# Expert stage of a hybrid encoder layer: plain fp32 products in 64-row blocks in place of split products in 80-row blocks, a ring of six weight sets, the residual kept in SBUF

## The reference, cut to what matters

```python
D_MODEL, N_GROUPS, EXPERTS_PER_GROUP, TOP_K, D_EXPERT = 1024, 4, 8, 2, 256
...
x = x + mix                                   # x2 below
t = rmsnorm(x, norm2_g).reshape(-1, D_MODEL)  # 576 rows
lg = t @ w_rg + b_rg                          # group; the best one is taken
le = t @ w_re + b_re                          # experts; the best two of that group
combine = ...                                 # (576, 32), two entries per row
def step(acc, xs):
    wg, wu, wd, c = xs                        # (1024,256) (1024,256) (256,1024)
    hdn = jax.nn.silu(t @ wg) * (t @ wu)
    return acc + c[:, None] * (hdn @ wd), None
x = x + acc
y = rmsnorm(x, final_g)
```

## Time and profile before

| | |
|---|---|
| median of 3 executions | 1424.2 us (1412.7 to 1426.9) |
| span of the profiled execution, its only time shown | 1420.8 us |
| PE busy | 1264.7 us, 89% of the span |
| DVE, ACT, POOL busy | 796.2, 616.8, 67.5 us |
| read from and written to HBM | 181.3 and 31.0 MB |

### The profile page before, as it was taken

The page is one execution under the profiler, slowest core; times in us unless marked ns, Lnnn a source line. Parts: engine busy times, 40 slices in busy tenths (PEclk is TensorE's granted clock), DMA queues, the critical chain, the costliest instruction groups (busy, mean ns, idle before and its releaser), DMA issues.

```text
span 1420.8 us, 22301 instructions
## 1 busy us (share of the span) xinstructions
PE 1264.7 (89%) x8549; PEld 1130.7 (80%) x8549; DVE 796.2 (56%) x938; ACT 616.8 (43%) x819; POOL 67.5 (5%) x132
## 2 busy tenths in 40 slices
PE   5989999999999999999989989982788888888880
PEld 4989999999999999999989989982455555555550
DVE  4437374473755736547365444326567677677645
ACT  5434243343433434335343222232566666666632
POOL 0001010010100101001010000003000000000002
PEclk9999999999999999999999999965799999999995
DMA  5261121211121112121102235533888888888836
GB/s 186 95 208 54 58 71 61 72 47 61 65 67 56 61 61 65 53 71 61 63 22 80 80 103 164 211 136 127 293 319 322 321 323 325 316 329 328 313 126 220
DMA packets 49434, 212.80 MB, mean 150 GB/s; under 512 B 5920, under 2 KB 8496, under 8 KB 37104
## 3 DMA queue, kind: packets, MB, share of 16 engines
q1 hardware_dynamic: 41200, 194.05, 39.2%
q0 software_dynamic: 2928, 10.05, 2.1%
q10 hardware_dynamic: 5264, 8.13, 1.6%
HBM read 181.25 MB, written 30.96 MB: 149 GB/s over the span
## 4 chain that ended last, share of the span: by engine, by line
PE 78%; DVE 7%; ACT 6%; DMA 4%; issue 3%; POOL 1%; SPq 0%; ACTq 0%; DVEq 0%; POOLq 0%
PE proj L620 25%; PE proj L1337 15%; PE wideB L1358 6%; PE proj L987 5%; PE wideA L378 4%; PE proj L930 3%; PE wideB L370 3%; PE wideB L384 2%; PE wideA L1324 2%; DVE xbl L1426 2%; ACT xbh L1422 2%; PE small L987 2%; DMA wraw<-in_w_in 1%; PE small L1178 1%; POOL scr_rows L1783 1%
## 5 line engine op out<-in xcount | busy, mean ns | idle before, releaser
L620 PE MATMUL proj<-xnh,whi 128*128 128x288 f32 x1152 | 347.9, 302 | 11.1 <-DVE xnl L1868 6.3
L620 PE MATMUL proj<-xnl,whi 128*128 128x288 f32 x1152 | 347.2, 301 | 0.0
L620 PE MATMUL proj<-xnh,wlo 128*128 128x288 f32 x1152 | 347.0, 301 | 0.0
L620 PEld LDWEIGHTS proj<-xnh,whi 128*128 128x128 f32 x1152 | 217.9, 189 | 12.3 <-issue 5.7
L1414 DVE TENSOR_TENSOR elo<-eraw,ehi 128x4096 fp32r<-128x4096 f32 x64 | 214.6, 3354 | 19.8 <-ACT ehi L1404 19.8
L620 PEld LDWEIGHTS proj<-xnl,whi 128*128 128x128 f32 x1152 | 217.8, 189 | 0.0
L620 PEld LDWEIGHTS proj<-xnh,wlo 128*128 128x128 f32 x1152 | 217.8, 189 | 0.0
L1337 PE MATMUL proj<-ehi,xbh 128*80 128x512 f32 x256 | 111.0, 433 | 33.9 <-DVE xbl L1426 33.9
L632 DVE TENSOR_TENSOR wlo<-wraw,whi 128x1024 fp32r<-128x1024 f32 x72 | 95.1, 1321 | 58.1 <-ACT whi L628 57.1
L1404 ACT ACTIVATE ehi<-eraw 128x4096 fp32r<-128x4096 f32 x32 | 116.1, 3627 | 0.5
L1337 PE MATMUL proj<-elo,xbh 128*80 128x512 f32 x256 | 109.9, 429 | 0.0
(11 more groups left out here) (329 smaller groups left out, 2370.2 us busy)
## 6 DMA issues: line engine op xcount, KB each, us to landing
wraw<-in_w_in SPq DMA_DIRECT2D x72, 512.0 KB, 3.3
eraw<-in_w_gate SPq DMA_DIRECT2D x32, 1024.0 KB, 4.9
eraw<-in_w_up SPq DMA_DIRECT2D x32, 1024.0 KB, 7.2
eraw<-in_w_down SPq DMA_DIRECT2D x32, 1024.0 KB, 5.5
wraw<-in_w_out SPq DMA_DIRECT2D x24, 512.0 KB, 3.7
xb<-scr_rows SPq DMA_DIRECT2D x32, 320.0 KB, 6.0
scr_y<-yout SPq DMA_DIRECT2D x32, 320.0 KB, 5.7
scr_gate<-gate ACTq DMA_DIRECT2D x16, 288.0 KB, 2.1
```

Source lines behind the costliest of these rows:

```text
L620: mm = pe.matmul(out, w[:, kc, :], x[:, kc, hh * HALF:(hh + 1) * HALF], start=(j == 0), stop=(j == 23))
```

## The change

The expert stage is rewritten; phases 1 to 3 keep their computation.

- Products are plain fp32 on the weights as loaded: per block 8 products for gate and up and 4 for down. All splitting of weights, rows and hidden values is gone; ACT copies the turned rows (`xT`), DVE the turned hidden values (`hT`).
- `BR` is 64 in place of 80. Rows and results of a block are 64 x 1024; `OVER`, the highest number of further blocks, is 17 in place of 14. The turned rows of two blocks have a place of their own in `wideA`.
- Six weight sets (`ring`) and three row buffers (`XB`). Sets 0 to 2 are loaded in phase 2, ahead of the last output weights, sets 3 and 4 at its end, set 5 behind the routing; set b mod 6 is loaded again when down of its block is done.
- `x2` stays in SBUF: its store and its five loads are gone, and the `scr_x2` array with them. Results are stored from ACT's queue.
- On PE, down of block b-1 follows the whole gate and up of block b.

```diff
-BR = 80
+BR = 64
+RING, XB = 6, 3
...
+        ring = []
+        for r, start in enumerate((0, EW, AT_RING2, AT_RING3, AT_W0, AT_P3)):
...
+            ring.append(sb(p4, f"ring{r}", [P, EW]))
...
-            weights_low(dve, 0, 0, 0)
-            weights_low(dve, 0, 0, 1)
...
+        def rows_turned(pe, b, k, x, arrived=None):
...
+            for c in range(KC):
+                mm = pe.transpose(wideA[:, 512 * k + c * BR:512 * k + (c + 1) * BR], v[:, c, :], ident[0:BR, 0:BR])
             mm.then_inc(e_xt, 1)
...
-            pe.wait_ge(e_low, 2 * b + 1)
-            pe.wait_ge(e_xl, b + 1)
+            pe.wait_ge(*(arrived or (e_w[r], 48 * (b // RING) + 48)))
+            pe.wait_ge(e_xc, b + 1)
             wait(pe, e_hid, b - 1)
...
+            for c in range(KC):
+                mm = pe.matmul(proj[k][0:BR, :], xT[k][:, c, :], w[:, :, c, :], start=(c == 0), stop=(c == KC - 1))
             mm.then_inc(e_gu, 1)
...
+            for c in range(2):
+                for n in range(2):
+                    at_w = GU + c * D + HALF_D * n
+                    mm = pe.matmul(wideB[0:BR, HALF_D * n:HALF_D * (n + 1)], hT[k][:, c, :],
+                                   ring[r][:, at_w:at_w + HALF_D], start=(c == 0), stop=(c == 1))
             mm.then_inc(e_dn, 1)
...
         def phase4_scalar(act):
...
+            rows_copied(act, 0, 0)
+            for b in range(EXPERTS):
+                silu_gate(act, b, b % 2)
+                if b > 0:
+                    y_copy(act, b - 1, (b - 1) % 2)
+                if b + 1 < EXPERTS:
+                    rows_copied(act, b + 1, (b + 1) % 2)
+                if b > 0:
+                    y_store(act, b - 1, (b - 1) % 2)
...
+            for r in range(3):
+                weights_load(r, r, e_w[r])
             sp.wait_ge(m_low, KC)
...
+            sp.wait_ge(route, ROUTE_STEPS)
+            weights_load(5, 5, e_w[5])
+            for b in range(1, EXPERTS):
+                if b + RING - 1 < EXPERTS:
+                    r = (b - 1) % RING
+                    sp.wait_ge(e_dn, b)
+                    weights_load(b + RING - 1, r, e_w[r])
+                if b + XB - 1 < EXPERTS:
+                    rows_load(b + XB - 1, (b - 1) % XB)
...
             def further(j):
...
-                sp.wait_ge(e_y, j + EXPERTS)
-                sp.dma_start(xb[0][0:BR, :], scr_rows[at(r, BR), :]).then_inc(o_x, 16)
-                gate_up_load(e, 0, o_w)
-                down_load(e, 0, o_w)
...
+                sp.wait_ge(e_dn, j + EXPERTS)
+                sp.dma_start(xb[LAST_X][0:BR, :], scr_rows[at(r, BR), :]).then_inc(o_x, 16)
+                weights_load(e, LAST_R, o_w)
```

More of the change, by code:

```diff
@@ L214, in encoder_layer @@
         a2.close()
-        a2 = area(AT_GD)
-        x2 = sb(a2, "x2", [P, UNITS, D])
+        a2 = area(AT_ML)
         ml = sb(a2, "ml", [P, KC, TOK], F32R)
         tg = [sb(a2, f"tg{k}", [P, TOK]) for k in range(2)]
-        mix = [sb(a2, f"mix{k}", [P, TOK]) for k in range(2)]
+        mix = [sb(a2, "mix0", [P, TOK]), None]
+        a2.close()
+        a2 = area(AT_G2)
+        mix[1] = sb(a2, "mix1", [P, TOK])
         a2.close()
@@ L223, in encoder_layer @@
         a2.close()
+        a2 = area(AT_X2)
+        x2 = sb(a2, "x2", [P, UNITS, D])
+        a2.close()
+        p4 = area(AT_YA)
+        xb = [sb(p4, f"xb{k}", [P, D]) for k in range(XB)]
+        xT = [sb(p4, f"xT{k}", [P, KC, BR]) for k in range(2)]
+        yout = [sb(p4, "yout0", [P, D]), None]
+        p4.close()
+        p3 = area(AT_G2)
+        g2row = sb(p3, "g2row", [P, D])
+        p3.close()
+        p3 = area(AT_YA)
+        tn = sb(p3, "tn", [P, UNITS, D])
+        p3.close()
         p3 = area(AT_P3)
-        g2row = sb(p3, "g2row", [P, D])
         wr = sb(p3, "wr", [P, KC, GROUPS + EXPERTS])
-        tn = sb(p3, "tn", [P, UNITS, D])
         tT = [sb(p3, f"tT{k}", [P, D]) for k in range(2)]
@@ L772, in encoder_layer @@
         spread_rows = sem("spread_rows")
[L773 to L776, removed]
+        e_w = [sem(f"e_w{r}") for r in range(RING)]
+        e_x = [sem(f"e_x{k}") for k in range(XB)]
+        e_xt, e_xc, e_gu, e_silu, e_hid, e_ht, e_hc, e_dn, e_y = (
+            sem("e_" + k) for k in "xt xc gu silu hid ht hc dn y".split())
         e_out = [sem("e_out0"), sem("e_out1")]
@@ L1380, in phase4_tensor @@
         def phase4_tensor(pe):
-            rows_turned(pe, 0, 0)
-            expert_tensor(pe, 0, 0, first=True)
-            expert_tensor(pe, 1, 1)
-            with pe.Fori(1, EXPERTS // 2 - 1) as i:
-                for k in range(2):
-                    expert_tensor(pe, 2 * i + k, k)
-            expert_tensor(pe, EXPERTS - 2, 0)
-            expert_tensor(pe, EXPERTS - 1, 1, last=True)
-            down(pe, EXPERTS - 1, 1)
+            rows_turned(pe, 0, 0, 0)
+            for b in range(EXPERTS):
+                gate_up(pe, b, b % 2, b % RING)
+                if b > 0:
+                    down(pe, b - 1, (b - 1) % 2, (b - 1) % RING, b - 1)
+                if b + 1 < EXPERTS:
+                    rows_turned(pe, b + 1, (b + 1) % 2, (b + 1) % XB)
+                hidden_turned(pe, b, b % 2)
```

302 lines of the change are left out of this document (102 added, 200 removed).

## The result

The changed kernel takes 1482.9 us (median of 4 executions, 1478.7 to 1484.1), the kernel before 1423.5 in the same comparison: 1.042 times as long, 95% interval 1.038 to 1.047. The forecast was slower, 1461 us, range 1363 to 1472. The direction is right; the size, +59 us and not +37, lies outside the range. The kernel before takes 1412 to 1415 us in some executions and 1420 to 1428 in the others, so differences of some ten us between medians are read with care.

What follows compares the result with a forecast made beforehand. PE and its wait for ACT and DVE were taken to set the stage, transfers close behind. Terms 11 - 3.9 - 1.0 + 5.7 + 25.1 gave +36.9, span 1457.7, median 1461 us, range 1363 to 1472.

Steps and rivals of the forecast that it cites:

- The price: Plain fp32 products on PE: 0.427 us an instruction at full clock, 24 instructions or 10.24 us a block.
- The stage, +5.7: The 32 expert blocks: products, 1.8 us gaps between blocks and a cold start give 387.2 us against 381.5, transfers hidden.
- rival 1: Expert stage: products cost 0.23 us an instruction on 64 columns, transfers set the block, 1375 us; chance 0.40.
- The further block, +25.1: Behind the 32nd block: 64 rows make exactly one more block necessary, its load, products and copies adding 25.1 us.
- Phase 2, +11: PE's output products wait for the 19th output weight, landing at 898 to 900 behind three weight sets: +11 us.
- Scatter and first rows, -4.9: Ahead of the stage: DVE's subtractions fall away, saving 3.9 us in POOL's scatter and 1.0 before the first gate and up.
- x2 and the end: x2's store and loads were off the chain: 0; copy, store, gather and weighted sum keep their form: 0, at most +2.

Runs made afterwards that it cites:

- all four edits: Changed kernel with rows ahead of weights, turning ahead of down, sets 0 to 2 behind the output weights, and blocks of 80 rows: 1393.1 us, 0.978.
- the run with half of the products and rows first: Changed kernel with half of the products left out (results wrong) and rows asked for ahead of weights in SP's queue: 1384.8 us, 0.975.
- Rows ahead of weights: Changed kernel with the rows of block b+2 asked for ahead of the weights of block b+5 in SP's queue: 1468.3 us, 1.032.
- The run with 128 partitions: Changed kernel with the further blocks' zeros written at the same place of SP's queue from 128 partitions instead of 64: 1473.8 us, 1.035.
- with 72 rows: Changed kernel with rows ahead of weights, turning ahead of down, sets 0 to 2 behind the output weights, and blocks of 72 rows: 1427.5 us, 1.004.
- rows turned earlier: Kernel before with rows of block b+1 turned between the halves of gate and up, ahead of down: 1398.6 us, 0.980.
- late sets: Changed kernel with weight sets 0 to 2 loaded behind the last output weights instead of ahead of the 19th: 1470.1 us, 1.033.

## Why the prediction was right in direction and too small

- **The price** was right. 0.43 us an instruction, on 64, 72 and 80 columns alike. The rival sentence from the Trainium skill, "TensorEngine Tiling (Array Packing)", Theoretical Speedup (up to 2x at 64 columns or fewer), is about tiles side by side; the one stream of this kernel gets nothing from 64 columns: 16 instructions take 6.89 us on 64 (1096.84 to 1103.73, the changed kernel) and 6.87 on 80 (1103.32 to 1110.19, all four edits).
- **The stage, +5.7, measured +25.4: the step that failed.** The forecast said "Transfers need 7.5 + 0.8 x 2.9 = 9.75 us in a block of 12.0, so they are hidden". It compared amounts. (The amount was short too: 10.6 - 7.5 is 3.1 and not 2.9, which makes 10.0, and the run with half of the products and rows first shows 10.4; 12 us would have hidden either.) The rows' place in the queue decided: behind a set that is asked for only one block ahead of the rows' use, with a round of 13.4 us where a block has 12.25. The prediction names this order itself, but only in rival 1. Rows ahead of weights takes back 13.0 of the 19.7 us missed. The other 6.7 are sizes: 24 x 0.429 = 10.30 us of products and 1.94 between them, where 10.24 and 1.8 were taken.
- **The further block, +25.1, measured +29.3.** The right block, too short a price: 11.9 us from the end of the last down product to the first product (10.2 were taken), and down at a lower clock (5.35 and not 3.4). Hiding the load takes 9.0 from it (5.9 from the median; the stage of that run starts later).
- **Phase 2, +11, measured +5.3.** The wait itself was +14.1 (910.55 less 868.52, before 892.07 less 864.16): the 19th weight landed at 908.2, not at 898 to 900. 4.4 of these 8 to 10 us are the late start of phase 2; the stretch from 885 to 910 moved 383 GB/s, where 422 were taken. Behind the wait 8.8 us came back, mainly 10.4 at the router, whose products and turnings ran near full clock, less 1.8 in the first products behind the wait (8.40 us for 6.63 before). That was in no step, so that this part came out below its forecast is luck.
- **Not in the forecast at all: +4.4 in phase 1**, which was taken for untouched. `BR` also sets how many partitions the zeros are written from. The run with 128 partitions shows that the wait is theirs. It accounts for 3.0 of the 4.4 us (7.7 for 4.7), and so do the profiles: with 64 rows and these zeros at their place PE is 91.4 to 92.0 us busy at 50 to 150 (eight profiles), with 80 rows 94.5 to 94.8 (four). The rest lies within what profiles with the same rows differ by: the products of the table's first row start at 866.9 to 870.2 in those eight, at 864.2 to 867.2 in those four. Fewer partitions alone do not explain the wait, for with 72 rows it is the longest of all, 10.4 us (PE 88.9 us busy, the products at 872.5). What sets it stayed open.
- **Scatter and first rows, -4.9, measured -4.6.** Without DVE's subtraction POOL's issues take 0.9 to 1.3 us each. From the first of them to the last transfer pass 12.1 us (986.07 to 998.12), before 15.9 (976.38 to 992.31): 3.9 less, as forecast. The other 0.7, where 1.0 was taken, lie between there and the first product.
- **x2 and the end** were free, as forecast (+0.3).

## What to carry to other kernels

A transfer is hidden when its round is: from the event that releases its issue, through everything ahead of it in its queue, to its landing, against the time to its use; that the bytes fit into the period says little. Ask of a constant that a change touches (here the rows of a block) what else is shaped by it, in phases far away too. Before a bound is attacked with other arithmetic, look at what stands between the products: the order of one turning took 28 us from the kernel before, that of one turning and one load 23 from the changed one, with no product touched.

## What the runs showed of the hardware that was not expected

- Zeros to HBM from 64 partitions took 26.2 us for 4352 KB, from 80 23.6 for 4480, from 128 15.0 for 4096 (the 256 KB behind them 16.6), issue to landing in the same stretch. It is no steady law: with 72 partitions the landing is not in the profile, but PE's wait behind these zeros was the longest.
- Between groups of products with 64-wide operands and turnings of 64 rows, PE loaded the next operand only when the last product had left: 0.13 to 0.19 us a seam, nothing of it at 72 or 80, where the turned rows also lie otherwise.
- The router's products ran at half clock in three profiles (the kernel before, the same with rows turned earlier, late sets: 3.26 us for the first 16) and near full clock in the other thirteen (1.71 to 2.10), with similar work ahead; 8 us hang on it, with the turnings between them 10. What decides it stayed open. That the two groups of times of the kernel before, some ten us apart, are the same thing is not shown.
